# Negated scores, inverted gates, VectorE for all low parts and for even heads, and the last two down units by halves

## The chip, the cores and the metric

The kernel runs on one core of a Trainium2 chip. Its metric is the device time of one execution in microseconds (us). The engines are TensorE (PE: matmul; PEld is its weight load), VectorE (DVE), ScalarE (ACT), GpSimd (POOL) and the SyncE queue (SP), which only issues DMAs here. They run on their own and meet at semaphores.

## The reference

Two transformer blocks over 256 tokens of width 1024, all in f32. What the change touches:

```python
def masked_softmax(s, mask):
    s = jnp.where(mask, s, -1e30)
    m = jnp.max(s, axis=-1, keepdims=True)
    p = jnp.where(mask, jnp.exp(s - m), 0.0)
    return p / jnp.maximum(jnp.sum(p, axis=-1, keepdims=True), 1e-30)

# first block, 16 heads of 64; three branches (compressed, selected, window)
s = q @ k * scale + rel_bias[bucket(distance)]          # per branch
o = g[0] * (p_cmp @ v_cmp) + g[1] * (p_slc @ v_slc) + g[2] * (p_win @ v_win)
# with g = sigmoid(h @ w_gates), one value per token, branch and head
v = a * sigmoid(gate); v = depthwise conv of width 31 (v) + b     # beside it
# first block also: cross attention (4 heads of 256), a gated feed-forward layer
# second block: spatial gating, 8 heads of 64 with rope and a log-count mask,
# then 128 x 128 experts, 16 for each of 8 heads of a token:
x = x + sum over them of (gate * gelu(h @ expert_u[e])) * expert_v[e]
return rms_norm(x, final_norm_g)
```

## The kernel before

**Weights.** The kernel is a stream of 467 weight units, each 128 x 1024 f32 (512 KB), in the order of use. A ring of 4 slots holds them. SyncE loads unit u when the low part of unit u-3 is made (L328-336). ScalarE rounds it to a high part in fp32r (`ring_hi`, L1134-1139), VectorE subtracts it from the raw unit for a low part (`ring_lo`, `lo`, L1662-1669), and TensorE multiplies three times: high by high, and the two mixed products (`three`, L369-372; by rows L443-445). All activations are split in the same way (`operand_hi`, `operand_lo`).

**Who makes the low parts.** Seven units of the convolution's and q's stage (SHARED: 4 of `uconv`, 2 of `q`, 1 of `ks`) have columns 256 to 1023 of their low part made by GpSimd (`shared_lo`, L1032-1036); VectorE waits for it (`pool_lo`) and makes 256. Seven units of the gates' projections (WHOLE) are multiplied unrounded in f32 (L382) and need no low part: VectorE touches one column of them to keep the count.

**Order.** There is no scheduler: each engine's queue is written out by hand, stage after stage: memory's keys, `uconv` (16 units), `kc`, `vc`, `q`, `ks`, `kw`, the gates, `v`; then 16 units of output gates beside the 16 heads; `xv`, the convolution's and the attention's output, cross attention, feed-forward; the second block; 128 units of `expert_u` and 128 of `expert_v`; the last norm and the store.

**Convolution.** VectorE multiplies the gated values (`glu`, L1754) and makes 240 tap operations of 128 x 256 (one channel chunk of 8 and one of 30 offsets each, `tap`, L1765), spread over its queue by `some_taps(count)`: 4 behind each low part from unit `uconv`+6 on, and 6 in the steps in which a SHARED unit's low part comes up. The rest lies between the steps of the heads.

**Heads.** A loop over 8 pairs. TensorE transposes the weighted probabilities of the even head (`nsa_transposes`, L548-556, waits for `scaled`), makes the scores of the next pair (L528-541), half a gate unit, the odd head's transposes, the other half, the values (L572, L576) and a WHOLE unit (L382). VectorE adds the bias and takes the row maxima of a head (`nsa_bias`, six operations, L1792), negates them (L1809) after both banks are read, makes a low part and taps, and after ScalarE's six exponentials (`nsa_exp`, L1276-1285, which waits for that negation) turns the row sums into scales (`nsa_scale`, L1815-1818: floor, reciprocal, times gate). Heads 1 to 13 are weighed by GpSimd (L1062-1072, six operations each), heads 0, 14 and 15 by VectorE (`nsa_weigh`, L1828). GpSimd also issues the loads of the bias rows and of the second half of memory (L1075), and adds up the convolution's chunks.

**Elsewhere.** Cross attention (`x_max`, L1960-1964) and the second block's attention (`bias2`, L2116-2126) have the same negation. In the second block GpSimd scales the 8 chunks of xT by a gain (L1106) and by the row norm (L1109), 16 operations of 128 x 256; VectorE waits for them at L2197. The last stage is 128 down units (`expert_down`, L984-997) into four banks, two for each 128 rows; after the last, ScalarE squares a row block (`fin_squares`, L1640), VectorE adds, ScalarE takes the root, VectorE inverts and scales (L2354), and SyncE stores the block's 512 KB (L349).

## Time and profile before

| | |
|---|---|
| median of 3 runs | 1551.72 us (1549.52 to 1553.7) |
| profiled execution, its own time | 1551.92 us |
| its span in the trace | 1549.3 us |
| TensorE busy | 1516.1 us (98%) |
| VectorE busy | 1144.1 us (74%) |
| ScalarE busy | 813.0 us (52%) |
| GpSimd busy | 320.2 us (21%) |
| TensorE's granted clock | 9 (90% or more of full speed) in each of 40 slices |

The span is the time from the first to the last recorded instruction of one execution; the own time is what the runs measure, for that same execution. The trace is read by instruction: start, duration, engine, line of the kernel, the buffers written and read, and in brackets the idle time of the engine before it and who ended that. Rows that follow each other from one line are joined, with their count. Successive matmuls overlap, and so do VectorE's operations by some 0.08 us: the distance of two starts (the pitch) is what one of them costs.

### The profile page before, as it was taken

What the parts mean: (1) busy time and instruction counts of PE and PEld (TensorE: products, weight loads), DVE (VectorE), ACT (ScalarE), POOL (GpSimd) and SP (SyncE); (2) the same over time, 40 slices, a digit from 0 to 9 for tenths busy, and PEclk for the clock granted to TensorE, in tenths of its full rate; (3) what the DMA queues carried; (4) which work ended last, traced back from release to release, by engine and by line L of the source; (5) the groups of instructions that cost most, each with busy time, mean ns of one, the idle gap of its engine ahead of it and who ended that gap; (6) DMA issues with size and microseconds to landing.
All of it is one profiled execution on the core that took longest, in us unless ns stands there. A gap on an engine that the chain in (4) does not pass through costs nothing.

```text
span 1549.3 us, 30948 instructions
## 1 busy us (share of the span) xinstructions
PE 1516.1 (98%) x10782; PEld 1408.9 (91%) x10782; DVE 1144.1 (74%) x2383; ACT 813.0 (52%) x1456; POOL 320.2 (21%) x422
## 2 busy tenths in 40 slices
PE   8999899999999999999999999999999999999998
PEld 7998777999999998789999999999999888888886
DVE  5799888765666666867999986888888665666564
ACT  6544778654544446565655564333334445544554
POOL 2220562000100000300000005888885000000000
PEclk9999999999999999999999999999999999999999
DMA  7574433544565554533555555444445665555553
GB/s 263 172 222 148 133 107 123 170 163 134 164 202 181 182 182 145 168 110 109 168 187 177 190 188 165 137 145 139 136 139 160 195 195 191 191 192 197 192 190 108
DMA packets 70859, 257.79 MB, mean 166 GB/s; under 512 B 8272, under 2 KB 8480, under 8 KB 70528
## 3 DMA queue, kind: packets, MB, share of 16 engines
q1 hardware_dynamic: 67824, 246.97, 48.7%
q0 software_dynamic: 2960, 9.86, 2.1%
q8 instruction: 42, 0.69, 0.2%
q14 instruction: 33, 0.27, 0.1%
HBM read 254.67 MB, written 1.08 MB: 165 GB/s over the span
## 4 chain that ended last, share of the span: by engine, by line
PE 82%; DVE 10%; ACT 4%; issue 2%; POOL 1%; DMA 0%; DVEq 0%; ACTq 0%
PE bank L370 17%; PE bank L371 17%; PE bank L372 17%; PE bank L993 7%; PE bank L994 7%; PE bank L992 7%; DVE arena L1765 4%; PE bank L971 4%; DVE ring_lo L1668 3%; POOL arena L1071 1%; ACT ring_hi L1139 1%; PE bank L459 1%; ACT arena L1283 1%; PE bank L554 1%; DVE arena L1792 0%
## 5 line engine op out<-in xcount | busy, mean ns | idle before, releaser
L1668 DVE TENSOR_TENSOR ring_lo<-ring_raw,ring_hi 128x1024 fp32r<-128x1024 f32 (+1 forms) x459 | 558.1, 1219 | 182.8 <-ACT ring_hi L1139 174.7
L370 PE MATMUL bank<-operand_hi,ring_hi 128*128 128x256 f32 x2144 | 618.5, 288 | 14.0 <-DVE ring_lo L1727 7.5
L371 PE MATMUL bank<-operand_lo,ring_hi 128*128 128x256 f32 x2144 | 606.9, 283 | 0.0
L372 PE MATMUL bank<-operand_hi,ring_lo 128*128 128x256 f32 x2144 | 606.8, 283 | 0.0
L1139 ACT ACTIVATE ring_hi<-ring_raw 128x1024 fp32r<-128x1024 f32 x459 | 480.2, 1049 | 80.3 <-PE bank L372 66.2
L370 PEld LDWEIGHTS bank<-operand_hi,ring_hi 128*128 128x128 f32 x2144 | 411.3, 192 | 18.0 <-DVE ring_lo L1727 7.5
L371 PEld LDWEIGHTS bank<-operand_lo,ring_hi 128*128 128x128 f32 x2144 | 411.7, 192 | 0.3
L372 PEld LDWEIGHTS bank<-operand_hi,ring_lo 128*128 128x128 f32 x2144 | 411.2, 192 | 0.0
L1123 POOL TENSOR_SCALAR onehots<-iota_k,routeT 128x128 f32<-128x128 f32 x256 | 207.5, 827 | 230.3 <-ACT routeT L1587 193.9
L992 PE MATMUL bank<-ring_hi,hidden_hi 128*128 128x512 f32 x512 | 199.2, 389 | 0.0
L993 PE MATMUL bank<-ring_lo,hidden_hi 128*128 128x512 f32 x512 | 199.2, 389 | 0.0
L994 PE MATMUL bank<-ring_hi,hidden_lo 128*128 128x512 f32 x512 | 199.2, 389 | 0.0
L1597 ACT ACTIVATE hidden_hi<-arena 128x256 fp32r (+1 forms) x128 | 53.5, 418 | 171.4 <-PE bank L994 171.0
L2315 DVE TENSOR_TENSOR hidden_lo<-arena,hidden_hi 128x256 fp32r<-128x256 f32 x128 | 54.5, 426 | 84.5 <-ACT hidden_hi L1597 84.0
L992 PEld LDWEIGHTS bank<-ring_hi,hidden_hi 128*128 128x128 f32 x512 | 96.1, 188 | 20.1
L994 PEld LDWEIGHTS bank<-ring_hi,hidden_lo 128*128 128x128 f32 x512 | 96.1, 188 | 19.8
L993 PEld LDWEIGHTS bank<-ring_lo,hidden_hi 128*128 128x128 f32 x512 | 96.1, 188 | 19.8
L1765 DVE SCALAR_TENSOR_TENSOR arena<-arena 128x256 f32<-128x256 f32 x240 | 110.9, 520 | 0.2
L1610 ACT ACTIVATE arena<-bank 128x252 f32<-128x252 f32 (+62 forms) x63 | 17.5, 278 | 148.5 <-PE bank L372 148.5
L370 PE MATMUL bank<-hidden_hi,ring_hi 128*128 128x256 f32 x256 | 72.7, 284 | 0.1
L371 PE MATMUL bank<-hidden_lo,ring_hi 128*128 128x256 f32 x256 | 72.4, 283 | 0.0
L372 PE MATMUL bank<-hidden_hi,ring_lo 128*128 128x256 f32 x256 | 72.4, 283 | 0.0
(301 smaller groups left out, 1751.3 us busy)
## 6 DMA issues: line engine op xcount, KB each, us to landing
ring_raw<-in_stream SPq DMA_DIRECT2D x467, 512.0 KB, 3.5
arena<-bias_rows POOLq DMA_DIRECT2D x8, 384.0 KB, 4.2
arena<-in_memT SPq DMA_DIRECT2D x2, 512.0 KB, 5.0
arena<-in_xT POOLq DMA_DIRECT2D x1, 1024.0 KB, 8.0
arena<-in_w POOLq DMA_DIRECT2D x2, 512.0 KB, 9.1
arena<-in_memT POOLq DMA_DIRECT2D x1, 1024.0 KB, 5.3
out_rows<-arena SPq DMA_DIRECT2D x2, 512.0 KB, 2.6
arena<-arena POOLq DMA_DIRECT2D x4, 128.0 KB, 4.7
```

The costliest lines, as they stand in the source:

```text
L370: pe.matmul(out, wh, xh, start=start, stop=False, **kw)
L371: pe.matmul(out, wh, xl, start=False, stop=False, **kw)
L372: return pe.matmul(out, wl, xh, start=False, stop=stop, **kw)
L971: m = pe.matmul(bank[6 + q][:, j * NEXP:(j + 1) * NEXP], hot[:, q, j, :], row_hot[q][j], start=True, stop=True)
L992: pe.matmul(o, h_hi[:, par, t0], w_hi[:, slot, n0], start=False, stop=False, skip_group_check=True)
L993: pe.matmul(o, h_hi[:, par, t0], w_lo[:, slot, n0], start=False, stop=False, skip_group_check=True)
L994: m = pe.matmul(o, h_lo[:, par, t0], w_hi[:, slot, n0], start=False, stop=last, skip_group_check=True)
L1123: ins = pool.tensor_scalar(hot[:, q, j, :], iota_k[:], routeT[:, 1, token], None, ALU.is_equal)
L1139: act.activation(dst, raw[:, slot, :], ACT.Copy).then_inc(hi_ready, 1)
L1668: dve.tensor_tensor(w_lo[:, slot, 0:n], raw[:, slot, 0:n], (raw if n == 1 else w_hi)[:, slot, 0:n].bitcast(F32), ALU.subtract)\
L1765: dve.scalar_tensor_tensor(cacc[:, c, :], vconv[:, c, k:k + S], dw[:, c, k:k + 1], cacc[:, c, :], ALU.mult, ALU.add)\
L2315: dve.tensor_tensor(h_lo[:, par, :], wall[:, bass.ds(n, 1), :].rearrange("p a t -> p (a t)"), h_hi[:, par, :].bitcast(F32), ALU.subtract). ...
```

## The change

Six edits, in one version:

- The scores come out negated (q is scaled by a negative factor, masks and biases are negated), so that a minimum stands where the maximum did and is already the negated maximum that the exponential wants, whose scale is -1. The negations fall away, and ScalarE waits for the freed banks instead.
- The gates are inverted once (128 x 96); a head's scales are (floored sum x inverted gate), then the reciprocal: two operations.
- SHARED and `shared_lo` are gone: VectorE makes all low parts whole, and 4 taps stand where 6 stood.
- VectorE weighs the even heads, GpSimd the odd ones 1 to 13. Taps in the loop are 2 + 4 + 3 + 5 a pair, where they were 2 + 3 + 3 + 4.
- Block 2's scaling of xT is 8 operations of VectorE in the value phase, with the row norm and the gain in one.
- The last two down units are multiplied bank by bank (3 + 3 matmuls), each bank is reported when it is full, squared at once, and each half row block is stored by a DMA of its own (256 KB).

```diff
--- before
+++ after
@@ -31,8 +31,8 @@
 EPS = 1e-6
-NEG = -1e30
-MAX_FLOOR = -1e29
+FAR = 1e30
+MIN_CEILING = 1e29
 G, R, HD = 4, 4, 64
...
@@ -296,8 +294,6 @@
         WHOLE = [U["gattn"] + n for n in range(2, 16, 2)]
-        SHARED = [U["uconv"] + 6, U["uconv"] + 9, U["uconv"] + 12, U["uconv"] + 15, U["q"] + 3, U["q"] + 6, U["ks"] + 1]
-        SHARE = 256
         FIRST_USE = [U[n] for n in ("xk", "uconv", "xv", "pwout", "pwout", "xq", "xo", "ffn", "va", "wout2", "wq2", "expert_u")]
@@ -345,9 +341,11 @@
             for t in range(TT):
-                sp.wait_ge(fin_out, t + 1)
-                sp.dma_start(out_d[t * P:(t + 1) * P, :], fin[:, t, :]).then_inc(stored, 16)
-            sp.wait_ge(stored, 16 * TT)
+                for half in range(2):
+                    n0 = slice(half * 512, (half + 1) * 512)
+                    sp.wait_ge(fin_out, 2 * t + half + 1)
+                    sp.dma_start(out_d[t * P:(t + 1) * P, n0], fin[:, t, n0]).then_inc(stored, 16)
+            sp.wait_ge(stored, 32 * TT)
@@ -981,27 +979,40 @@
-            def expert_down(u, slot, n, par, last=False):
+            def down_half(slot, par, t, half, last=False):
+                t0 = slice(t * P, (t + 1) * P)
+                n0 = slice(half * 512, (half + 1) * 512)
+                o = bank[2 * t + half][:, :]
+                pe.matmul(o, h_hi[:, par, t0], w_hi[:, slot, n0], start=False, stop=False, skip_group_check=True)
+                pe.matmul(o, h_hi[:, par, t0], w_lo[:, slot, n0], start=False, stop=False, skip_group_check=True)
+                return pe.matmul(o, h_lo[:, par, t0], w_hi[:, slot, n0], start=False, stop=last, skip_group_check=True)
+
+            def expert_down(u, slot, n, par):
                 pe.wait_ge(lo_ready, u + 1)
...
                 for t in range(TT):
-                    t0 = slice(t * P, (t + 1) * P)
                     for half in range(2):
-                        n0 = slice(half * 512, (half + 1) * 512)
-                        o = bank[2 * t + half][:, :]
-                        pe.matmul(o, h_hi[:, par, t0], w_hi[:, slot, n0], start=False, stop=False, skip_group_check=True)
-                        pe.matmul(o, h_hi[:, par, t0], w_lo[:, slot, n0], start=False, stop=False, skip_group_check=True)
-                        m = pe.matmul(o, h_lo[:, par, t0], w_hi[:, slot, n0], start=False, stop=last, skip_group_check=True)
-                    if last and t == 0:
+                        m = down_half(slot, par, t, half)
+                m.then_inc(unit_done, 1)
+
+            def last_two(u, n):
+
+                for t in range(TT):
+                    for half in range(2):
+                        for k in range(2):
+                            if t == 0 and half == 0:
+                                pe.wait_ge(lo_ready, u + k + 1)
+                                pe.wait_ge(ehid_ready, n + k + 1)
+                            m = down_half((u + k) % RING, (n + k) % 2, t, half, last=k == 1)
                         m.then_inc(fin_bank, 1)
-                m.then_inc(unit_done, 1)
...
                     expert_down(i * RING + (u0 + k), (u0 + k) % RING, i * RING + k, k % 2)
-            for n in range(NEXP - RING, NEXP):
-                expert_down(u0 + n, (u0 + n) % RING, n, n % 2, last=n == NEXP - 1)
+            for n in range(NEXP - RING, NEXP - 2):
+                expert_down(u0 + n, (u0 + n) % RING, n, n % 2)
+            last_two(u0 + NEXP - 2, NEXP - 2)
@@ -1029,12 +1040,6 @@
-            def shared_lo(u):
-
-                s, c = u % RING, slice(SHARE, D)
-                pool.wait_ge(hi_ready, u + 1)
-                pool.tensor_tensor(w_lo[:, s, c], raw[:, s, c], w_hi[:, s, c].bitcast(F32), ALU.subtract).then_inc(pool_lo, 1)
-
             bias_rows(0)
@@ -1072,7 +1073,9 @@
                 if hh == NH - 2:
-                    pool.wait_ge(biased, NH)
+                    for b in (1, 0):
+                        emptied(pool, ("s", b, NH - 1))
+                        emptied(pool, ("s", b, NH - 2))
                     pool.dma_start(mem2, memT_d).then_inc(mem2_in, 16)
@@ -1100,13 +1103,6 @@
                 pool.dma_start(lnv[:, n, :], lnv_d[n:n + 1, :].to_broadcast([P, 512])).then_inc(lnv_in, 16)
-
-            pool.wait_ge(rows_scale, 1)
-            for c in range(KC):
-                pool.tensor_scalar(xT[:, c, :], xT[:, c, :], cols[:, G_FINAL, c:c + 1], 1.0, ALU.mult, ALU.mult).then_inc(pool_seq, 1)
-            for c in range(KC):
-                pool.wait_ge(pool_seq, 3 + c)
-                pool.tensor_tensor(xT[:, c, :], xT[:, c, :], std[:], ALU.mult).then_inc(rows_scaled, 1)
@@ -1251,7 +1247,7 @@
             for j in range(8):
-                copy_cols("q", j, qT[:, j, :], scale=HD ** -0.5)
+                copy_cols("q", j, qT[:, j, :], scale=-HD ** -0.5)
             for name, dst in (("ks", ksT), ("kw", kwT)):
@@ -1275,12 +1271,13 @@
                 s = hh % 2
-                act.wait_ge(biased, hh + 1)
+                for b in (1, 0):
+                    emptied(act, ("s", b, hh))
                 for k in parts:
...
                     v = prob[:, s, 384 * b + n0:384 * b + n1]
-                    ins = act.activation(v, v, ACT.Exp, bias=mx[:, s, k:k + 1], accum_out=sums[:, s, k:k + 1])
+                    ins = act.activation(v, v, ACT.Exp, bias=mx[:, s, k:k + 1], scale=-1.0, accum_out=sums[:, s, k:k + 1])
                 if 5 in parts:
@@ -1503,10 +1500,10 @@
                 s = h % 2
-                act.wait_ge(s2_biased, h + 1)
+                emptied(act, ("s2", h))
                 for t in range(TT):
                     v = prob2[:, s, t * S:(t + 1) * S]
-                    ins = act.activation(v, v, ACT.Exp, bias=mx[:, s, t:t + 1], accum_out=sums[:, s, t:t + 1])
+                    ins = act.activation(v, v, ACT.Exp, bias=mx[:, s, t:t + 1], scale=-1.0, accum_out=sums[:, s, t:t + 1])
                 ins.then_inc(s2_exp, 1)
@@ -1639,6 +1636,7 @@
                 for half in range(2):
+                    act.wait_ge(fin_bank, 2 * t + half + 1)
                     ins = act.activation(fsq[:, t, half * 512:(half + 1) * 512], bank[2 * t + half][:, :], ACT.Square,
@@ -1647,10 +1645,8 @@
-            act.wait_ge(fin_bank, 1)
             fin_squares(0)
             fin_std(0)
-            act.wait_ge(unit_done, UNITS)
             fin_squares(1)
@@ -1662,9 +1658,6 @@
                 n = 1 if isinstance(u, int) and u in WHOLE else D
-                if isinstance(u, int) and u in SHARED:
-                    dve.wait_ge(pool_lo, SHARED.index(u) + 1)
-                    n = SHARE
                 dve.tensor_tensor(w_lo[:, slot, 0:n], raw[:, slot, 0:n], (raw if n == 1 else w_hi)[:, slot, 0:n].bitcast(F32), ALU.subtract)\
@@ -1779,7 +1772,7 @@
                 if u >= U["uconv"] + 6:
-                    some_taps(6 if u + RING - 1 in SHARED else 4)
+                    some_taps(4)
@@ -1789,7 +1782,7 @@
                 def with_bias(out, scored, distances, n):
-                    return dve.tensor_tensor_reduce(out, scored, distances, 1.0, MAX_FLOOR, ALU.add, ALU.max, mx[:, s, n:n + 1])
+                    return dve.tensor_tensor_reduce(out, scored, distances, 1.0, MIN_CEILING, ALU.add, ALU.min, mx[:, s, n:n + 1])
@@ -1804,18 +1797,14 @@
                 ins.then_inc(bank_free[2 * s], 1)
-                for b in (1, 0):
-                    emptied(dve, ("s", b, hh))
-                dve.tensor_scalar(mx[:, s, :], mx[:, s, :], -1.0, None, ALU.mult).then_inc(biased, 1)
...
                 dve.wait_ge(exped, hh + 1)
-                after(dve.tensor_scalar(rinv[:, s, :], sums[:, s, :], 1e-30, None, ALU.max))
-                after(dve.reciprocal(rinv[:, s, :], rinv[:, s, :]))
-                r3 = rinv[:, s, :].rearrange("p (b t) -> p b t", b=3)
-                dve.tensor_tensor(r3, r3, gates[:, :, hh, :], ALU.mult).then_inc(scale_ready, 1)
+                r3, s3 = (v[:, s, :].rearrange("p (b t) -> p b t", b=3) for v in (rinv, sums))
+                after(dve.scalar_tensor_tensor(r3, s3, 1e-30, gates[:, :, hh, :], ALU.max, ALU.mult))
+                dve.reciprocal(rinv[:, s, :], rinv[:, s, :]).then_inc(scale_ready, 1)
@@ -1837,6 +1826,7 @@
             emptied(dve, ("gates", "turned"))
+            after(dve.reciprocal(gates, gates))
             nsa_scale(0)
@@ -1850,18 +1840,17 @@
                 lo_to(U["gattn"] + 2 * pair + 1 + RING)
-                some_taps(3)
+                some_taps(4)
                 if pair + 1 < NH // 2:
                     nsa_scale(2 * pair + 2)
-                    if 2 * pair + 2 == NH - 2:
-                        nsa_weigh(NH - 2)
+                    nsa_weigh(2 * pair + 2)
                 some_taps(3)
...
                     lo_to(U["gattn"] + 2 * pair + 2 + RING)
-                some_taps(4)
+                some_taps(5)
             some_taps(KC * (CONV_W - 1))
@@ -1954,14 +1943,13 @@
                 b, _ = filled[("xq", j)]
-                dve.scalar_tensor_tensor(qT[:, j, :], bank[b][:, 0:S], XHD ** -0.5, std[:], ALU.mult, ALU.mult)\
+                dve.scalar_tensor_tensor(qT[:, j, :], bank[b][:, 0:S], -XHD ** -0.5, std[:], ALU.mult, ALU.mult)\
                    .then_inc(bank_free[b], 1)
...
                 dve.wait_ge(xs, h + 1)
-                after(dve.tensor_reduce(mx[:, s, 0:TT], bank[6][:, :].rearrange("p (a b) -> p a b", a=TT), AX, ALU.max))
-                dve.tensor_scalar(mx[:, s, 0:TT], mx[:, s, 0:TT], -1.0, None, ALU.mult).then_inc(xs_max, 1)
+                dve.tensor_reduce(mx[:, s, 0:TT], bank[6][:, :].rearrange("p (a b) -> p a b", a=TT), AX, ALU.min).then_inc(xs_max, 1)
@@ -2065,9 +2053,8 @@
             dve.wait_ge(col_std, 3)
-            dve.tensor_scalar(pcolq, pcol, HD2 ** -0.5, None, ALU.mult).then_inc(col_std, 1)
-            emptied(dve, ("norm", N_2))
-            dve.reciprocal(std[:], std[:]).then_inc(rows_scale, 1)
+            dve.tensor_scalar(pcolq, pcol, -HD2 ** -0.5, None, ALU.mult).then_inc(col_std, 1)
+            rstd(("norm", N_2))
             lo_to(U["q2"] + 1 + RING)
@@ -2120,10 +2107,8 @@
                     ins = dve.tensor_tensor_reduce(prob2[:, s, t * S:(t + 1) * S], bank[4 + s][:, t * S:(t + 1) * S], lc[:, t, :],
-                                                   1.0, -3e38, ALU.add, ALU.max, mx[:, s, t:t + 1])
+                                                   1.0, 3e38, ALU.add, ALU.min, mx[:, s, t:t + 1])
                 ins.then_inc(bank_free[4 + s], 1)
-                emptied(dve, ("s2", h))
-                dve.tensor_scalar(mx[:, s, 0:TT], mx[:, s, 0:TT], -1.0, None, ALU.mult).then_inc(s2_biased, 1)
@@ -2181,6 +2166,8 @@
                         bias2(h)
+                for c in (2 * j, 2 * j + 1):
+                    dve.scalar_tensor_tensor(xT[:, c, :], xT[:, c, :], cols[:, G_FINAL, c:c + 1], std[:], ALU.mult, ALU.mult)
                 if j == 0:
@@ -2194,7 +2181,6 @@
             mix_lo(1)
-            dve.wait_ge(rows_scaled, KC)
             tail_rest("wout2", wout2_bank, O_PEER, G_NORM2)
@@ -2351,8 +2337,8 @@
                     n0 = slice(half * 512, (half + 1) * 512)
-                    ins = dve.scalar_tensor_tensor(fin[:, t, n0], bank[2 * t + half][:, :], rinv[:, 0, t:t + 1], fg[:, n0], ALU.mult, ALU.mult)
-                ins.then_inc(fin_out, 1)
+                    dve.scalar_tensor_tensor(fin[:, t, n0], bank[2 * t + half][:, :], rinv[:, 0, t:t + 1], fg[:, n0], ALU.mult, ALU.mult)\
+                       .then_inc(fin_out, 1)
```

## Rows read from the trace of the kernel before

**Rows 1.** the page, busy time by engine: us, share of span, instructions

```profile
PE 1516.1 (98%) x10782; PEld 1408.9 (91%) x10782; DVE 1144.1 (74%) x2383; ACT 813.0 (52%) x1456; POOL 320.2 (21%) x422
```

**Rows 2.** TensorE's waits: line, releaser and its line: us, times, longest

```profile
PE bank L554 <- POOL arena L1071: 4.8, 5, 1.6
PE bank L370 <- DVE ring_lo L1668: 3.4, 3, 1.5
PE bank L370 <- DVE arena L1754: 2.4, 3, 1.0
PE bank L443 <- DVE ring_lo L1668: 1.7, 2, 1.3
PE bank L443 <- DVE operand_lo L1707: 1.5, 1, 1.5
PE bank L537 <- ACT arena L1304: 1.0, 1, 1.0
PE bank L572 <- ACT arena L1312: 0.9, 2, 0.5
```

**Rows 3.** VectorE by line, 58 to 158 us: count, busy, mean ns, idle before

```profile
L1765 DVE SCALAR_TENSOR_TENSOR arena<-arena 128x256 f32<-128x256 f32 x143 | 64.8, 515 | 0.2
L1668 DVE TENSOR_TENSOR ring_lo<-ring_raw,ring_hi 128x1024 fp32r<-128x1024 f32 (+1 forms) x29 | 30.4, 1048 | 7.7 <-POOL ring_lo L1036 4.3 <-ACT ring_hi L1139 3.4
```

**Rows 4.** busy us by engine in one pair: PE, PEld, DVE, ACT, POOL

```profile
191.00:204.00 13.00, 12.37 (x100) 10.26 (x98) 10.54 (x46) 9.75 (x33) 7.22 (x13) 1.00 0.35 112
```

**Rows 5.** timeline of TensorE, block 2: start, duration, instruction, idle before

```profile
632.06 0.39 PE L445 MATMUL bank<-ring_hi,operand_lo 128*128 128x512 f32 x1
633.73 0.50 PE L443 MATMUL bank<-ring_hi,operand_hi 128*128 128x512 f32 x1 [1.29 <-DVE ring_lo L1668]
```

**Rows 6.** timeline of VectorE, 65 to 70 us

```profile
65.47 2.80 DVE L1765 SCALAR_TENSOR_TENSOR arena<-arena 128x256 f32<-128x256 f32 x4
68.20 0.41 DVE L1668 TENSOR_TENSOR ring_lo<-ring_raw,ring_hi 128x256 fp32r<-128x256 f32 x1
68.53 1.66 DVE L1765 SCALAR_TENSOR_TENSOR arena<-arena 128x256 f32<-128x256 f32 x4
```

**Rows 7.** timeline of GpSimd, the same stretch

```profile
63.98 2.82 POOL L1036 TENSOR_TENSOR ring_lo<-ring_raw,ring_hi 128x768 fp32r<-128x768 f32 x1 [6.10 <-ACT ring_hi L1139]
```

**Rows 8.** timeline of TensorE, last scores of pair 0

```profile
147.58 0.52 PE L541 MATMUL bank<-arena 64*128 64x15 f32 x8
```

**Rows 9.** timeline of VectorE, heads 0 and 1

```profile
153.80 0.27 DVE L1792 CUSTOM_DVE_ANT_0 arena<-bank,arena 128x128 f32<-128x128 f32 x1
...
156.93 0.17 DVE L1809 TENSOR_SCALAR row_max<-row_max 128x6 f32<-128x6 f32 x1
...
158.16 0.17 DVE L1815 TENSOR_SCALAR row_scale<-row_sum 128x6 f32<-128x6 f32 x1
...
158.79 1.29 DVE L1828 TENSOR_SCALAR arena<-arena,row_scale 128x128 f32<-128x128 f32 x6
```

**Rows 10.** timeline of GpSimd, one pair of heads

```profile
200.30 6.96 POOL L1071 TENSOR_SCALAR arena<-arena,row_scale 128x128 f32<-128x128 f32 x12 [5.78 <-DVE row_scale L1818]
```

**Rows 11.** timeline of VectorE, the same pair

```profile
204.03 2.33 DVE L1765 SCALAR_TENSOR_TENSOR arena<-arena 128x256 f32<-128x256 f32 x4
```

**Rows 12.** timeline of GpSimd, block 2

```profile
622.70 9.29 POOL L1109 TENSOR_TENSOR arena<-arena,std 128x256 f32<-128x256 f32 x8
```

**Rows 13.** timeline of VectorE, block 2

```profile
627.62 1.76 DVE L1668 TENSOR_TENSOR ring_lo<-ring_raw,ring_hi 128x1024 fp32r<-128x1024 f32 x1
```

**Rows 14.** timeline of TensorE, the last matmul

```profile
1541.61 0.39 PE L994 MATMUL bank<-ring_hi,hidden_lo 128*128 128x512 f32 x1
```

**Rows 15.** timeline of VectorE, the end

```profile
1544.15 0.14 DVE L2349 TENSOR_TENSOR row_scale<-row_sum 128x1 f32<-128x1 f32 x1
```

**Rows 16.** timeline of ScalarE, the end

```profile
1543.07 0.59 ACT L1642 ACTIVATE arena<-bank 128x512 f32<-128x512 f32 x1
```

**Rows 17.** the page, DMA issues: KB each, us to landing

```profile
out_rows<-arena SPq DMA_DIRECT2D x2, 512.0 KB, 2.6
```

More of the change, by code:

```diff
@@ L202, in build @@
         first_half_hi, first_half_lo = sem("first_half_hi"), sem("first_half_lo")
-        lo_ready, pool_lo = sem("lo_ready"), sem("pool_lo")
+        lo_ready = sem("lo_ready")
         unit_done = sem("unit_done")
@@ L214, in build @@
         col_std = sem("col_std")
-        rows_summed, rows_scale, rows_scaled = sem("rows_summed"), sem("rows_scale"), sem("rows_scaled")
+        rows_summed = sem("rows_summed")
         silu_done = sem("silu_done")
@@ L233, in build @@
         scores = sem("scores")
-        biased = sem("biased")
         exped = sem("exped")
@@ L267, in build @@
         s2 = sem("s2")
-        s2_biased = sem("s2_biased")
         s2_exp = sem("s2_exp")
@@ L1045, in _ @@
                 pool.dma_start(z[kv][HD:P, G, 0:CMP_BLOCK - 1], pos_d[kv][:, 1:CMP_BLOCK]).then_inc(w1_in, 16)
-            for u in SHARED[:4]:
-                shared_lo(u)
             for kv, (name, src) in enumerate((("kc", kcT), ("vc", vcT))):
@@ L1058, in _ @@
                 pool.dma_start(w1[:, kv, :, :].rearrange("p a b -> p (a b)"), w1_d[kv]).then_inc(w1_in, 16)
-            for u in SHARED[4:7]:
-                shared_lo(u)
             for hh in range(NH):
                 s = hh % 2
-                if 0 < hh < NH - 2:
+                if s and hh < NH - 1:
                     pool.wait_ge(scale_ready, hh + 1)
@@ L1226, in _ @@
                     act.wait_ge(brow_done, 1)
-                    act.activation(brow[0:NH, S:2 * S], bank[2][0:NH, 0:S], ACT.Copy).then_inc(bank_free[2], 1)
+                    act.activation(brow[0:NH, S:2 * S], bank[2][0:NH, 0:S], ACT.Copy, scale=-1.0).then_inc(bank_free[2], 1)
                 if j == 4:
@@ L1388, in x_exp @@
                     ins = act.activation(xprob[:, s, t * S:(t + 1) * S], bank[6][:, t * S:(t + 1) * S], ACT.Exp,
-                                         bias=mx[:, s, t:t + 1], accum_out=sums[:, s, t:t + 1])
+                                         bias=mx[:, s, t:t + 1], scale=-1.0, accum_out=sums[:, s, t:t + 1])
                 ins.then_inc(bank_free[6], 1)
@@ L1735, in _ @@
             dve.wait_ge(onehot_in, 32)
-            dve.memset(brow[0:NH, 0:S], NEG).then_inc(brow_sb, 1)
+            dve.memset(brow[0:NH, 0:S], FAR).then_inc(brow_sb, 1)
             dve.wait_ge(consts_in, 48)
@@ L2426 @@
     seen = (np.abs(q - k) <= 64).astype(int) + ((q - k) % 4 == 0) + ((q - k) % 16 == 0)
-    lc = np.where(seen > 0, np.log(np.maximum(seen, 1)), NEG).astype(np.float32).reshape(TT, P, S).transpose(1, 0, 2)
+    lc = np.where(seen > 0, -np.log(np.maximum(seen, 1)), FAR).astype(np.float32).reshape(TT, P, S).transpose(1, 0, 2)
     inv = (1.0 / (np.float32(10000.0) ** (np.arange(0, HD2, 2, dtype=np.float32) / np.float32(HD2)))).astype(np.float32)
```

## The prediction

> **What bounds the kernel now.** I read the page first: TensorE is busy for 1516.1 of the span of 1549.3 us [rows 1], so all that a change beside it can give back lies in the 33 us in which it is not. The profiled execution's own time is 1551.92 us, 2.6 us more than its span and 0.2 us above the median of 1551.72; the sum is made against it. Then the list of TensorE's waits [rows 2], which says who ended them: VectorE's low parts (L1668) and gated products (L1754), GpSimd's weighing (L1071, five times), and small ones on ScalarE behind them. Then VectorE by line for the 100 us from 58 to 158: it stood idle for 7.9 us, 4.3 of them behind GpSimd's parts [rows 3]; and busy time in one pair of attention heads: 10.54 of 13.00 us [rows 4]. So VectorE is full in the convolution's stage, and in the head loop it has some 2 us a pair to spare while GpSimd is late.
>
> A wait costs more than its row: the matmul after 632.06 starts 1.67 us later where the pitch is 0.23, so 1.44 us for an idle row of 1.29 [rows 5]. I add 0.15 us to each.
>
> **GpSimd's three quarters of seven low parts go to VectorE.** Each such step adds 768 columns. A quarter part costs 0.33 us (68.20 to 68.53 [rows 6]), a whole one 1.15 (it is all that stands between the negation at 156.93, a slot of 0.08, and the scale at 158.16 [rows 9]): 7 x 0.82 = +5.7 us. Against this, four taps beside GpSimd's operation of 2.82 us [rows 7] take 2.80 us and four alone 1.66 [rows 6]; the stage's 143 taps fill 64.8 us [rows 3], where at 1.66 for four they would fill 59.3: -5.5. The 4.3 us of idle time behind GpSimd's parts go. Six steps make 4 taps for 6: 12 taps x 0.40 = -4.8 us, moved behind. Together VectorE reaches the heads some 9 us earlier in its own work. How late is it today? TensorE issued the last scores of pair 0 at 147.58, VectorE took them up at 153.80 [rows 8, 9]: 5.7 us after they were there (0.5 us for the row itself), busy all the while. 9 covers 5.7, so VectorE is then at TensorE's heels and not behind it. So the waits of 100 to 158 us go: L1754 three times (2.4 + 0.45) and L1668 into L370 three times (3.4 + 0.45) [rows 2]: **-6.7 us**. The next two belong to the same lateness, since ScalarE's exponentials of pair 0 stood behind that bias: L1304 1.0, L572's first 0.5, with 0.3: **-1.8 us**. Bounds for both: 0 if VectorE is still late, 8.5.
>
> **Even heads' weights on VectorE, odd ones on GpSimd.** Today GpSimd does both heads of a pair in 6.96 us from 200.30, after 5.78 us idle [rows 10] and 0.7 us for a DMA's issue: a pair takes 13.45 us, and TensorE comes to the even head before GpSimd is done with it. VectorE does a head in six operations, 1.29 us with a pitch of 1.20 [rows 9]. Nothing of GpSimd stands before the even transposes then, and the odd head (about 3.1 of the 6.96) starts with its own scale, before the even one is through today. The five waits go: 4.8 + 0.75 = **-5.6 us**.
>
> What that costs VectorE per pair: +1.20 weighing, +0.79 (2 taps of the 12 moved, 0.40 each, plus none in the last pair), -0.36 for two negations (0.17 each [rows 9]; one slot of the pitch), -0.40 for two scales with two operations in place of three (0.63 us for three, 158.16 to 158.79 [rows 9]). Taps beside GpSimd's weighing last 2.33/4 = 0.58 [rows 11] against 0.40; with GpSimd at work for 3.1 instead of 7 us half of that goes, -0.4. Sum +0.8 to +1.2 on some 11.3 us of work (10.54 in 13.00 is 10.9 in 13.45 [rows 4], with 0.4 of gaps too short to use), so 12.1 to 12.5. TensorE without its wait needs 13.45 - 1.0 = 12.4 us. Both engines are then full, and where the taps fall just ahead of a bias or a scale, the chain bias, exponential, scale, weights comes later. I charge 0.15 us a pair, **+0.9 us**, for waits of the values (L572) or transposes, against **-0.6** for the one of today that has no other term (0.41 + 0.15; L572 stands twice, 0.9 [rows 2]). Bounds: 0 (the 1.0 us by which L1668's and the scales' idle time shrinks absorbs it) to 1.0 us a pair, 6 us, if VectorE's 12.5 grows to 13.4. The nearest row is the busy one, 10.54 of 13.00 [rows 4], so the value is near the lower end.
>
> The Trainium skill bears on this. "SBUF: State Buffer", section "Who interferes with whom", says that VectorE with two SBUF inputs and GpSimd share a port pair that one of them holds for a whole instruction, the loser waiting. Of the taps beside the low parts the trace agrees (2.80 for 1.66); beside the weighing it shows 2.33 for four, so no full block. By the page's rule the three taps or so a pair that still meet a weighing of some 0.6 us each would lose 0.3 us more each, an estimate of some 6 us in all and a time of 1540.
>
> **Negated scores and inverted gates.** The 16 + 4 + 8 negations vanish; ScalarE's exponential starts about 0.18 us sooner in each of 28 chains. It is on the path only where ScalarE waited, priced above. Inverting gates adds one reciprocal of 96 columns once, 0.35 us, ahead of the first scale; VectorE's lead covers it. GpSimd's load of the second memory block waits for freed banks instead of a count that rose 0.2 us later: nothing.
>
> **Cross values.** L443 on L1707, 1.5 us once: VectorE comes out of the loop with 3 taps left and not 5, 0.8 us earlier, less its smaller spare time: **-0.5** (0 to -1.6).
>
> **Block 2.** GpSimd's 16 operations run to 632 (622.70 + 9.29) [rows 12], and a low part beside them takes 1.76 us [rows 13], where one between other operations has a pitch of 1.15 [rows 9]. Over the 619 to 632 stretch three low parts at +0.3 to +0.5, four products slowed by 0.4 each and two scalings make about 4 us of VectorE. It was late by 1.3 and 0.5 us (L443 on L1668, 1.7 [rows 2]), so these go with 0.3 and an unlisted slip of 0.3: **-2.3 us**. What comes in their place are 8 operations of about 0.40 us in the value phase (as a tap [rows 6]), 3.2 us against 8 negations (-1.4) in a stretch where VectorE has some 12 us idle in 50; the wait of L855 at 672.5 may grow, **+0.2** (0 to 1.5).
>
> **The end.** Today both halves of the second row block end together: last matmul at 1541.61 (over at 1542.00), two squares, sum at 1544.15 [rows 14, 15]: 2.15 us, the second square from 1543.07 and 0.59 long [rows 16], 0.5 us of the rest because ScalarE was still at the first block's root. By banks only one square stands behind the last matmul, started 0.1 us after it, and the sum comes at about 1544.15 - 1543.07 - 0.2 = 0.87 us: -1.3. The last DMA carries 256 for 512 KB; the row shows 2.6 us [rows 17], of which the bytes can be at most about half: -0.3 (0 to -1). But now the last two units start as one, and unit 127's hidden part is ready only about 0.5 us after they could start (its gate waits until unit 125 is over, and split and low part take 0.42 each): +0.5 (0 to 0.9). **-1.1 us.**
>
> The skill's page "DMA: Bandwidth & Descriptors", section "Anatomy of one DMA", prices a transfer as a fixed 2.0 us plus bytes over 436 GB/s; by that the half would save an estimated 0.6 us, the sum would be 0.3 lower. The row of 2.6 us is near it.
>
> **Sum.** -6.7 -1.8 -5.6 -0.6 +0.9 -0.5 -2.3 +0.2 -1.1 = -17.5 us: 1551.92 - 17.5 = **1534.4 us**, a span of 1531.8.
>
> **Rivals.**
> 1. VectorE becomes the bound of the head loop. For: 12.1 to 12.5 us of work against TensorE's 12.4. Against: 12.5 is the upper end. At 13.2 us a pair in seven pairs it gives back 5.6: 1540 us.
> 2. The convolution's stage stays late: the low parts are whole, 5.7 us, and the taps stay at today's mean of 0.45 us (64.8/143 [rows 3]), slowed by something else than GpSimd. For: only part of them stands beside it. Against: four at 1.66 right behind four at 2.80. Half of the 8.5 and the even head's spare time are lost: 1540.
> 3. Slower: the port. If VectorE's taps and low parts in the loop are held by GpSimd's odd weights as by L1036 (2.80 for 1.66, up to 1.6 us each), and GpSimd's pass stretches too, a pair needs more than 12.4 + 17.5/7 = 14.9 us, which is the point from which the change loses; at 15.7 us it is 7 x 3.3 - 17.5 = +5.6: 1557 us. Against: four taps beside weighing, 2.33.
> 4. Most goes as forecast, and TensorE finds another late partner in the loop, ScalarE (9.75 of 13.00 [rows 4]), with exponentials of both heads in a row: 0.5 us a pair, 1538.
>
> **Chances.** Forecast 0.62 (1531 to 1537.5), rival 4 0.13, rivals 1 and 2 0.09 each, rival 3 0.02, nothing gained 0.05 (the waits change their names only). Range 1530 to 1543. About 0.3%, 4.7 us, is what a measurement of this kernel can tell from no change: faster by more 0.93, within 0.04, slower 0.03.
>
> **What would show it.** In the list of TensorE's waits L1754, L1071 and L1668 into L370 are gone or under 1 us in all; VectorE's four taps at 65 us take 1.66; the first bias starts within 1 us of the scores' end; a pair is 12.4 to 12.6 us; L443 on L1668 near 633 us is gone; the last sum stands 0.9 us behind the last matmul, and TensorE has a gap of about 0.5 us at unit 126. Wrong it is if a pair stays above 13 us, or if VectorE is still 5 us late at the first bias.

## The result and the profile after

The changed kernel takes 1533.95 us (1533.54 to 1534.65, 4 runs) against 1552.71 for the one before (1549.52 to 1553.77, 4 runs): a ratio of 0.9883 with a 95% interval of 0.9867 to 0.9899. Forecast were 1534.4 us and a span of 1531.8; the span is 1532.0. A second set on another occasion gave 1534.60 us and 0.9878 (0.9861 to 0.9894).

TensorE's waits after, with who ended them (total, times, longest), answer to [rows 2]:

```profile
PE bank L570 <- ACT arena L1309: 1.5, 4, 0.8
PE bank L634 <- ACT arena L1340: 1.0, 1, 1.0
PE bank L441 <- DVE operand_lo L1700: 0.9, 1, 0.9
PE bank L853 <- ACT arena L1482: 0.7, 1, 0.7
PE bank L986 <- DVE hidden_lo L2301: 0.4, 1, 0.4
```

GpSimd is gone from the list, and so are the gated products and the low parts. What has grown stands on ScalarE: its copies in front of the values (L570, 0.9 before) and the convolution's squares (L634, 0.3 before). VectorE over 58 to 158 us, by line, and busy times (PE, PEld, DVE, ACT, POOL) in the convolution's stage and in one pair of heads answer to [rows 3, 4]:

```profile
L1758 DVE SCALAR_TENSOR_TENSOR arena<-arena 128x256 f32<-128x256 f32 x139 | 58.2, 484 | 0.2
L1661 DVE TENSOR_TENSOR ring_lo<-ring_raw,ring_hi 128x1024 fp32r<-128x1024 f32 x29 | 35.5, 1222 | 0.4
```

```profile
58.00:100.00 42.00, 42.00 (x352) 42.00 (x351) 41.79 (x80) 21.23 (x31) 6.52 (x11) 1.00 0.64 195
189.00:201.00 12.00, 12.00 (x100) 10.34 (x96) 11.58 (x49) 9.09 (x30) 4.74 (x7) 1.00 0.34 115
```

139 taps fill 58.2 us where 143 filled 64.8, and VectorE's idle time ahead of low parts fell from 7.7 to 0.4 us. From 58 to 100 us TensorE is busy all the time; the kernel before had in the same stretch:

```profile
58.00:100.00 42.00, 39.56 (x324) 38.83 (x323) 41.79 (x79) 19.67 (x29) 9.27 (x8) 1.00 0.53 166
```

VectorE's 41.79 us are the same in both: a tap that is held up counts as busy too, so VectorE's busy share does not show what was gained, and TensorE's does. In the loop VectorE is now busy for 11.58 of 12.00 us: it has become the second full engine there.

Where the 17.3 us of the span went is read from starts of the same matmul in both traces:

| matmul | before | after | gained so far |
|---|---|---|---|
| first product behind the scores of pair 0 | 158.48 | 151.45 | 7.0 |
| values of pair 0 | 169.99 | 161.29 | 8.7 |
| even transposes of the next pairs | 243.73 | 230.53 | 13.2 |
| cross values | 264.48 | 250.56 | 13.9 |
| behind block 2's late low parts | 637.20 | 621.33 | 15.9 |
| behind the first three matmuls of unit 126 (after the change that is unit 127's first) | 1537.08 | 1521.63 | 15.45 |
| end of the span | 1549.3 | 1532.0 | 17.3 |

Traces differ in the first 13 us, before any edit: the others lie up to 0.75 us from the changed kernel's, which is itself 0.46 later than the one before. In what follows this is taken out of every distance that is said to be "from the start of the convolution on"; with it the whole gain is 17.8 us and not 17.3.

### The profile page after: what moved, and what is told of

It is laid out like the page before. It is cut to its first block, busy times and chain, and to the rows that moved or that the text cites. A ratio compares the mean times of both kernels' runs of the same rounds, so it can differ in the third digit from the quotient of the medians.

```text
span 1532.0 us, 30888 instructions
## 1 busy us (share of the span) xinstructions
PE 1513.5 (99%) x10782; PEld 1409.8 (92%) x10782; DVE 1143.9 (75%) x2384; ACT 812.7 (53%) x1456; POOL 270.9 (18%) x363
## 4 chain that ended last, share of the span: by engine, by line
PE 90%; DVE 5%; ACT 3%; issue 1%; DMA 0%; DVEq 0%; ACTq 0%
PE bank L368 18%; PE bank L369 18%; PE bank L370 18%; PE bank L986 8%; PE bank L987 8%; PE bank L988 8%; PE bank L969 4%; DVE arena L1758 1%; PE bank L441 1%; DVE ring_lo L1661 1%; PE bank L442 1%; PE bank L443 1%; PE bank L457 1%; PE bank L380 1%; ACT ring_hi L1135 1%
## 5 line engine op out<-in xcount | busy, mean ns | idle before, releaser
L1661 DVE TENSOR_TENSOR ring_lo<-ring_raw,ring_hi 128x1024 fp32r<-128x1024 f32 x459 | 562.6, 1229 | 178.2 <-ACT ring_hi L1135 175.2
L1758 DVE SCALAR_TENSOR_TENSOR arena<-arena 128x256 f32<-128x256 f32 x240 | 106.1, 503 | 0.2
```

Source lines behind the costliest of these rows:

```text
L1661: dve.tensor_tensor(w_lo[:, slot, 0:n], raw[:, slot, 0:n], (raw if n == 1 else w_hi)[:, slot, 0:n].bitcast(F32), ALU.subtract)\
L1758: dve.scalar_tensor_tensor(cacc[:, c, :], vconv[:, c, k:k + S], dw[:, c, k:k + 1], cacc[:, c, :], ALU.mult, ALU.add)\
```

## The experiments

Each undoes or adds one part; the changed kernel took 1533.95 us in the first set and 1534.60 in the second. The first four experiments ran on a third occasion, without the changed kernel beside them and with 1553.49 us for the kernel before; so where single us matter, their traces decide and not their times.

### The low parts back on GpSimd (u_lo)

```diff
+ for u in SHARED: shared_lo(u)          # GpSimd, columns 256 to 1023
- some_taps(4); loop 2 + 4 + 3 + 5
+ some_taps(6 if u + RING - 1 in SHARED else 4); loop 2 + 3 + 3 + 4
```

> The changed kernel with one part undone: GpSimd makes three quarters of seven low parts again, 6 taps in those steps, 12 taps fewer in the head loop. Theory (GpSimd's operation holds VectorE up, and the lateness of the convolution's stage is carried into the heads): TensorE's waits on the gated products and low parts between 70 and 158 us come back (6.7 us), and those of ScalarE on the first pair (1.8); the lighter loop gives back about 1 of today's 1.5 us on the values. 1541 to 1543 us, and four taps beside GpSimd's operation take 2.8 us again. Rival (the stage was late for another reason, and another of the six edits mended it): below 1536 us.

1542.62 us, span 1540.3. VectorE's timeline and TensorE's waits:

```profile
65.97 2.81 DVE L1774 SCALAR_TENSOR_TENSOR arena<-arena 128x256 f32<-128x256 f32 x4
```

```profile
PE bank L370 <- DVE arena L1763: 2.5, 3, 1.0
PE bank L370 <- ACT arena L1305: 2.3, 1, 2.3
PE bank L370 <- DVE ring_lo L1677: 2.1, 3, 1.1
PE bank L537 <- ACT arena L1314: 1.2, 1, 1.2
```

The taps beside GpSimd's operation take 2.81 again, and the waits are back: the scores of pair 1 start at 165.20 for 155.50, 9.7 us later, of which the lighter loop returns 1.5. That is 1.0 us more than the change had gained up to there; most of it lies in the wait of 2.3 us, behind ScalarE's exponentials, at the place where the kernel before waited 1.5 us for a low part. The theory holds, the rival falls.

### Even heads back on GpSimd (u_heads)

```diff
-                if s and hh < NH - 1:
+                if 0 < hh < NH - 2:
-                    nsa_weigh(2 * pair + 2)
+                    if 2 * pair + 2 == NH - 2: nsa_weigh(NH - 2)
```

> The changed kernel with one part undone: GpSimd weighs the even heads 2 to 12 too; VectorE keeps 14 taps a pair. Theory (GpSimd's 7 us for two heads end too late for the even transposes): TensorE waits for GpSimd at five or six even heads, but 0.4 us less each than before the change since no negation and one operation less of the scale stand in the chain: 5 x 0.7 us, 1537 to 1539 us. Rival (the wait came from VectorE's late scale, which the earlier convolution's stage mended): no such wait, 1533 to 1535 us.

1537.57 us. The profiled execution is the slowest of the four (1539.47 us, span 1536.6), and 3.3 us of it are TensorE's clock and no wait (last section); the other three have spans of 1533.5 to 1534.3. From the start of the convolution to the convolution's squares it lost 1.95 us:

```profile
PE bank L552 <- POOL arena L1072: 2.2, 2, 1.6
PE bank L570 <- ACT arena L1309: 1.0, 3, 0.4
```

The time falls in the expected range, but not for the expected reason. GpSimd is waited for twice and not five times, at heads 2 and 10; with the other edits in place VectorE's weighing is worth 1.9 us, not 3.5. What sets those two apart is not that GpSimd came late to them: it had stood idle for 5.8 and 3.6 us. One of GpSimd's six operations for the head ran beside a whole low part of VectorE and took as long as that, 1.3 us. Here are such an operation (of 15 columns) and its low part in the kernel before, and then all six operations of the even head at which that kernel did not wait, where the low part (216.30) started only as the last of them was ending:

```profile
202.83 1.36 POOL L1071 TENSOR_SCALAR arena<-arena,row_scale 128x15 f32<-128x15 f32 x1
202.87 1.24 DVE L1668 TENSOR_TENSOR ring_lo<-ring_raw,ring_hi 128x1024 fp32r<-128x1024 f32 x1 [0.29 <-ACT ring_hi L1139]
213.73 2.69 POOL L1071 TENSOR_SCALAR arena<-arena,row_scale 128x128 f32<-128x128 f32 x6 [5.77 <-DVE row_scale L1818]
```

This sorts every even head from 2 to 12 that GpSimd weighs in the five traces that have such heads (before, b_lo, u_heads, mixed, mixed_early). A low part falls into 16 of the 26; these take 3.8 to 4.3 us, and TensorE waits at each of them. The other 10 take 2.6 to 2.8 us, and it waits at none.

### Negation and third scale operation back (u_small)

```diff
+                dve.tensor_scalar(mx[:, s, :], mx[:, s, :], 1.0, None, ALU.mult).then_inc(biased, 1)
-                after(dve.scalar_tensor_tensor(r3, s3, 1e-30, gates[:, :, hh, :], ALU.max, ALU.mult))
-                dve.reciprocal(rinv[:, s, :], rinv[:, s, :])
+                floor; reciprocal; times gates (not inverted)
```

> The changed kernel with two small parts undone in the 16 heads: an operation in the place of the negation (times 1, ScalarE waits for it), and the scale in three operations with gates not inverted. Theory (VectorE is full in the head loop after the change, idle for some 0.3 of 12.4 us a pair): 0.76 us a pair of added work makes TensorE wait 0.4 us a pair more, 1536 to 1537 us; the waits are on the values (ScalarE's copies) and on the even head's weights. Rival (VectorE's slack absorbs it): 1533.5 to 1534.5 us.

1539.83 us, span 1537.2, with no loss of clock:

```profile
PE bank L571 <- ACT arena L1309: 4.6, 6, 1.1
PE bank L442 <- DVE operand_lo L1700: 1.3, 1, 1.3
PE bank L553 <- POOL arena L1073: 1.1, 1, 1.1
```

Both ranges missed. From the start of the convolution on it loses 4.4 us up to the values of pair 6 (242.43 for 237.30, 0.75 of it from the first 13 us): 0.63 us a pair (seven of them) for 0.76 us of added work, so that VectorE's idle 0.3 us a pair absorbed little of it. These two small edits are worth 4.4 us, more than twice the weighing.

### Block 2's scaling back on GpSimd (u_block2)

```diff
+ pool: 8 x tensor_scalar(xT, gain), 8 x tensor_tensor(xT, std)
- dve:  8 x scalar_tensor_tensor(xT, gain, std) in the value phase
```

> The changed kernel with one part undone: GpSimd scales xT in the second block by 16 operations. Theory: the low parts beside them take 1.5 to 1.76 us again, the waits of rows on low parts near 617 to 622 us come back (2.3 us, with 0.2 us given back later): 1536 us. Rival (those waits came from elsewhere): 1534 us.

1537.31 us, 1.3 over the forecast. The wait of rows on low parts is exactly back; the trace puts 2.6 us there (the same matmul at 621.33 and 623.66, and 0.27 us of another start). The profiled execution is again the slowest of its four (1541.10 us, span 1537.7), with 3.3 us of the clock behind that; the other spans are 1534.1 to 1535.5, 2.1 to 3.5 over the changed kernel's:

```profile
PE bank L441 <- DVE ring_lo L1668: 1.7, 2, 1.3
```

### The changed kernel again (after_again)

> The changed kernel once more, as the measure for the others of this group on this chip. All theories: 1533.5 to 1535 us.

1534.60 us, span 1531.7, the same waits.

### The end undone (u_tail)

```diff
- last_two(u0 + NEXP - 2, NEXP - 2)      # bank by bank, 4 DMAs of 256 KB
+ expert_down(...) twice, last=True      # row block by row block, 2 DMAs of 512 KB
```

> The changed kernel with the end undone: the last two down units one after the other, row blocks reported whole, two DMAs of 512 KB. Theory: the gap of 0.54 us at unit 126 goes, from the last matmul to the last sum it is 2.15 us instead of 0.75, the last DMA takes 0.3 to 0.6 us more: 1.1 to 1.5 us over the changed kernel. Rival (the halves only move work): within 0.3 us of it.

1536.94 us against 1534.60, spans 1533.4 and 1531.7. The last matmul starts at 1525.74 and the sum stands 2.15 us behind its end:

```profile
1525.74 0.39 PE L990 MATMUL bank<-ring_hi,hidden_lo 128*128 128x512 f32 x1
```

```profile
1528.28 0.15 DVE L2321 TENSOR_TENSOR row_scale<-row_sum 128x1 f32<-128x1 f32 x1
```

With the 0.4 us taken out by which the first 13 us differ, the end is worth 1.4 us by the spans, inside the theory; the medians are 2.3 apart, in runs that scatter by 2 to 3 us.

### VectorE weighs all heads (all_dve)

```diff
- GpSimd: six tensor_scalar for each odd head
+                    nsa_weigh(2 * pair + 3)   # and nsa_weigh(1) ahead of the loop
```

> The changed kernel with VectorE weighing the odd heads too; GpSimd weighs none and keeps its place in the order. Theory (VectorE is full, and taps beside GpSimd's weighing take 0.53 for 0.40 us): VectorE gets 1.2 us a pair more and 0.7 us less from undisturbed taps, +0.5 us a pair on TensorE, 3 us in all, 1537 to 1538 us, and five taps take 2.0 instead of 2.75 us. Rival A (the port is held for whole operations of GpSimd, so that 4 us of its work cost more than 1.2): no change or faster. Rival B (taps are slow for another reason): taps stay at 0.53, +1.2 us a pair, 1541 us.

1542.28 us, span 1540.4. Five taps of the changed kernel beside GpSimd's weighing, and five here with GpSimd idle:

```profile
193.40 2.75 DVE L1758 SCALAR_TENSOR_TENSOR arena<-arena 128x256 f32<-128x256 f32 x5
```

```profile
200.37 2.06 DVE L1751 SCALAR_TENSOR_TENSOR arena<-arena 128x256 f32<-128x256 f32 x5
```

The part on the taps holds: 0.69 us of disturbance a pair, which the absence of GpSimd gives back, and both rivals fall on it. The time was missed by 4 to 5 us. 3.3 us of the span are TensorE's clock behind a wait of 2.8 us on the values of pair 1; the rest, 5.5 us, is for the most part waits on the values, 6.7 us in all for 1.5. VectorE weighs an odd head in 1.34 us, but head 3, just ahead of that wait, in 2.77:

```profile
167.79 2.77 DVE L1810 TENSOR_SCALAR arena<-arena,row_scale 128x128 f32<-128x128 f32 x6
182.00 1.34 DVE L1810 TENSOR_SCALAR arena<-arena,row_scale 128x128 f32<-128x128 f32 x6
```

GpSimd is at work beside heads 1, 3 and 9, which take 2.28, 2.77 and 2.77 us: the same scale that starts VectorE's weighing releases GpSimd for a bias row's issue and for its sums of the convolution. In those three pairs 4.4 of the 5.5 us are lost. So this run shows that the version is slower; it does not show that GpSimd's work for odd heads is worth its disturbance where the sums stand elsewhere, which was not tried.

### A better order (both_better)

```diff
-                    for half in range(2):
-                        for k in range(2):
+  t == 0: unit 126 into banks 0 and 1, then unit 127 into banks 0 and 1
-  taps 2 + 4 + 3 + 5
+  taps 3 + 4 + 3 + 4
```

> The changed kernel with two edits of the order: for the first row block the last two units are taken as unit 126 into both banks, then unit 127 (0.68 us of work in front of the hidden part that is late), and the loop's taps are 3 + 4 + 3 + 4 instead of 2 + 4 + 3 + 5, so that VectorE takes the even head's bias up one tap earlier. Theory: the gap of 0.54 us at unit 126 goes, and the waits on the values after pair 0 (3 x 0.4 us) go or halve since ScalarE's exponentials in front of the odd head's copies start 0.4 us earlier: 1.0 to 1.7 us less than the changed kernel beside it. Rival (VectorE is the bound in the loop, so that the order of its taps moves nothing): 0.5 us less.

1533.25 us (1532.61 to 1533.65) against 1534.60 (1533.54 to 1535.62), ratio to before 0.9867 (0.9850 to 0.9883); the intervals of the two overlap, so that the order of the two rests on the traces. There the gap at unit 126 is gone (from the unit's first matmul to the next unit's it is 0.68 us and not 1.22), and 0.3 us are gained up to the convolution's squares: the waits on the values fall from 1.5 to 1.3 only, and the squares' wait grows from 1.0 to 1.4. The end of the theory holds, the loop's part is nearer to the rival.

### One part alone on the kernel before (b_lo, b_heads)

> The kernel before with one part alone: VectorE makes all low parts whole, 4 taps in each step, loop 2 + 4 + 3 + 5. Theory (the convolution's stage is worth 8.5 us by itself, and lateness is not carried through the loop): the waits of 70 to 170 us go, GpSimd's five waits at even heads stay, and 2 taps more a pair cost nothing beside them: -8 us, 1545 to 1546 us. Rival (GpSimd's waits were lateness carried on): they fall too, 1541 to 1543 us.

> The kernel before with one part alone: VectorE weighs the even heads, GpSimd the odd ones; taps and low parts as before. Theory: GpSimd's five waits go (5.6 us); VectorE's 1.2 us a pair more fit into its 2 us of idle time, with waits on the values of some 0.3 us a pair: -4 us, 1549 to 1550 us; the waits of 70 to 170 us stay. Rival (VectorE's chain of bias, negation, exponential and scale becomes the bound as soon as GpSimd isn't): the loop gives back what it gained, -1 us or less, 1552 to 1554 us.

b_lo: 1548.72 us against 1553.86, ratio 0.9966 (0.9951 to 0.9982), span 1542.7. b_heads: 1549.98 us, 0.9975 (0.9964 to 0.9986), span 1546.1. In b_heads VectorE weighs the even heads and GpSimd the odd ones; the rest of both is the kernel before. TensorE's waits, first of b_lo, then of b_heads:

```profile
PE bank L554 <- POOL arena L1061: 6.7, 6, 2.6
```

```profile
PE bank L370 <- DVE ring_lo L1668: 3.6, 4, 1.5
PE bank L572 <- ACT arena L1312: 2.6, 5, 1.1
```

b_lo wins 9.2 us up to pair 0 and loses 2.5 of them in the loop, where GpSimd's wait grows from 4.8 to 6.7 (a low part now falls into head 8 as well, so it is waited for at six heads): it is no lateness carried on, so the rival falls. But the theory is met in part only: it had the waits unchanged and 8 us won. By span b_lo wins 6.6, by time 5.1. Three of its six executions have a mean granted clock of 0.996 and spans of 1546.7 to 1548.1; the two shortest, 1542.1 and 1542.7, have 0.998 and 0.999.

b_heads removes GpSimd's five waits, and a third of that comes back on the values (0.9 to 2.6 us); it wins 3.7 us from the start of the convolution on, as the theory had it. The two alone give 10.1 us from there on; with block 2 (2.6) and the end (1.4) that is 14.1 of 17.8. u_small, which has everything but the two small edits, wins 13.3. So the last 3.6 to 4.5 us need the small edits beside the others.

### Even heads on GpSimd but for two (mixed, mixed_early)

```diff
-                if s and hh < NH - 1:
+                if 0 < hh < NH - 2 and hh not in (2, 10):
```

> The changed kernel with the two edits of the order of before (last units; taps 3 + 4 + 3 + 4), and GpSimd weighing the even heads again, but heads 2 and 10, which stood behind its sums of the convolution: there VectorE does it. Theory (with all heads' weights on GpSimd only those two were late, 2.6 us, and VectorE, which is full, is relieved of 1.2 us a pair): 1531.5 to 1532.5 us, one to two below the changed kernel with the two edits. Rival (with the even head back GpSimd is late at more heads as TensorE's waits on the values go): 1534 us or more.

> The same with taps 4 + 4 + 3 + 3: one more in front of the odd head's bias, one less in front of the even one's. Theory (what the waits on the values follow is when the even head's bias starts): 0.3 to 0.8 us below the one with 3 + 4 + 3 + 4. Rival (the odd head's chain is then as late as the even one's was): the same or up to 1 us more.

1536.93 and 1536.94 us, spans 1534.5 and 1536.1: both slower than the version they start from (both_better), and both theories fall. TensorE waits at the even head of pair 2 (mixed, then mixed_early, which waits at that of pair 6 too):

```profile
PE bank L552 <- POOL arena L1074: 1.7, 1, 1.7
```

```profile
PE bank L552 <- POOL arena L1074: 3.5, 2, 2.6
```

The idea that GpSimd is late behind its sums of the convolution, from which I chose heads 2 and 10, is wrong: it had stood idle for 4 us before head 4. Heads 4 and 6 in mixed:

```profile
178.03 4.06 POOL L1074 TENSOR_SCALAR arena<-arena,row_scale 128x128 f32<-128x128 f32 x6 [4.04 <-DVE row_scale L1809]
193.05 2.79 POOL L1074 TENSOR_SCALAR arena<-arena,row_scale 128x128 f32<-128x128 f32 x6 [7.78 <-DVE row_scale L1809]
```

A low part (179.55, 1.33 us long) made one operation of head 4 last 1.44 us. Behind the wait the clock fell as well (last section), which costs 1.7 us in both. Apart from that spot mixed gains: 1.1 us from 183.4 to 250.6 us against the changed kernel. Another place for the low part was not tried.

## Why the prediction was right, point by point

- **The convolution's stage**, -6.7 forecast, -7.5 from its start to the matmul at 158.48; the first pair -1.8 forecast, -1.7 measured. The reason held too: four taps at 64 us take 1.67 for the 2.80 of [rows 6], and VectorE takes up the first bias at 143.84, 1.1 us behind the end of its scores (142.71) and not 5.7:

```profile
63.95 1.67 DVE L1758 SCALAR_TENSOR_TENSOR arena<-arena 128x256 f32<-128x256 f32 x4
```

- **GpSimd's five waits**, -5.6 forecast, gone. But the reason was incomplete and the share of the parts wrong. I had GpSimd late by the length of its pass; the rows show that it is late at the even heads into which a low part falls, and that about 1.1 us of such a pass is the one operation that is held up. Four of the five waits were shorter than that (0.7 to 0.9 us), the fifth was 1.6. I gave the gain all to the even heads' weights; u_heads shows that with the other edits in place only two of five waits return (1.9 us net). And the step that had negations and gates on the path only "where ScalarE waited" was too small: u_small has them at 4.4 us, since VectorE is full.
- **VectorE's load of the loop**, 12.1 to 12.5 us a pair forecast; over four pairs (180.25 to 230.53) it is busy for 49.05 of 50.28 us, 12.3 of 12.6. The odd head was mis-sized: 4.04 us on GpSimd, not 3.1, because the low part now falls into it, and its taps stay slow (2.75 for five, 0.55 each). It still ends in time:

```profile
192.28 4.04 POOL L1072 TENSOR_SCALAR arena<-arena,row_scale 128x128 f32<-128x128 f32 x6 [7.58 <-DVE row_scale L1807]
```

- **New waits on the values**, +0.9 forecast, and -0.6 for the one that was to go. There are four of 1.5 us in rows; in the starts of the matmuls they cost 0.8, 0.3 and 0.2, and at pair 4, where one stood before, a wait of 0.2 stays and 0.2 is won. That is +1.0 for +0.3, so these terms are 0.7 too small.
- **Cross values** -0.5: the wait fell from 1.5 to 0.9, and the next one grew from 0.3 to 1.0, which gave 0.66 back. I had not asked what is late next there: ScalarE's squares stand behind two sigmoids of 1.9 us.
- **Inverting the gates** took 0.75 us, not 0.35, without effect on TensorE.
- **Block 2**: -2.3 forecast, -2.6 measured (629.4 to 637.2), and u_block2 puts 2.6 back. The growth of L853's wait (+0.2) did not come: 0.7 both times.
- **The end**: -1.1 forecast, -1.3 measured with the new gap of 0.54 in it (0.5 forecast):

```profile
1521.63 0.47 PE L986 MATMUL bank<-ring_hi,hidden_hi 128*128 128x512 f32 x1 [0.38 <-DVE hidden_lo L2301]
```

```profile
1527.43 0.16 DVE L2335 TENSOR_TENSOR row_scale<-row_sum 128x1 f32<-128x1 f32 x1 [0.53 <-ACT arena L1640]
```

```profile
out_rows<-arena SPq DMA_DIRECT2D x4, 256.0 KB, 2.0
```

  The last matmul is over at 1526.68, so the sum stands 0.75 us behind it (0.87 forecast). The DMA of half the bytes takes 2.0 for 2.6 us: 0.6, twice my 0.3. The Trainium skill ("DMA: Bandwidth & Descriptors", "Anatomy of one DMA") gives its fit for DMAs that GpSimd issues; worked out from it, the two would take an estimated 2.6 and 3.2 us. These are SyncE's, and the rows have 2.0 and 2.6: the difference agrees, the level lies 0.6 us under it.

The values (0.7 us) and the squares (0.7) came out worse than forecast, the convolution's stage (0.8), block 2 (0.5), the cross values (0.2) and the end (0.2) better; with the 0.46 us of the first 13 us the span missed by 0.2. The mechanisms that carry most of the sum held, the closeness of it is partly luck. Rival 1 (VectorE the bound of the loop) was nearer than its 0.09: u_small shows that it begins at the changed kernel's own load. Rival 4 is the small waits that are left. Rivals 2 and 3 fell: the taps do fall to 0.42, and in the loop those beside the weighing take 0.55 (0.58 in pair 0). The prediction's estimate of 1540 us had three taps a pair lose 0.9 us more; five of them lose 0.69 together, and VectorE's 12.3 us a pair stay below the 12.6.

By medians of times the gain is 18.8 and 19.4 us, by the two traces' spans 17.3. The spans of the other executions are on record too: those of the kernel before lie at 1550.5 to 1552.9 in the second set (median 1551.2), those of the changed kernel at 1531.7 to 1532.8 in both (median 1532.0), which makes 19.2. So the traced execution of the kernel before, with 1549.3, was a short one. In the others its mean granted clock is 0.996 to 0.999, in the changed kernel's 0.999 to 1.000; a fall as in the last section leaves that mean at 0.998 or 0.999 and costs 1.7 to 3.3 us. Such falls behind waits that the change has removed would explain it, but no trace of such an execution was kept, so this is not shown.

## What to carry to other kernels

A wait that names an engine tells who came last, not what made it late: of GpSimd's six operations a head, look at each by itself and at what VectorE does beside it. Here one low part beside it made the pass 1.1 us longer, more than was missing at four of the five heads, and an order that keeps the two apart might do as much there as moving the work (not tried). Before work is moved to a helper's neighbour, count its load by the loop's period; at 98% (49.05 of 50.28 us) 0.76 us more of it made the loop 0.63 us longer. After each removed wait, write down which engine is next in that place (the squares behind the sigmoids here).

## What the runs showed of the hardware that I had not expected

TensorE's clock halves for some 3 to 7 us behind certain gaps, in kernels that are otherwise granted the full clock. In all_dve (start and end, length, busy, count, clock, DMA) it follows an idle stretch of 2.8 us and costs 3.3 us:

```profile
175.00:177.00 2.00, 0.00 (x0) 1.00 0.00 0
177.00:179.00 2.00, 1.84 (x18) 0.84 0.31 61
179.00:181.00 2.00, 2.00 (x7) 0.50 0.53 209
181.00:183.00 2.00, 2.00 (x7) 0.50 0.00 0
183.00:185.00 2.00, 2.00 (x6) 0.50 0.54 169
185.00:187.00 2.00, 2.00 (x15) 0.95 0.68 196
```

0.50 is the lower of the two levels, 1.2 for 2.4 GHz. In mixed and mixed_early it follows the waits of 1.7 and 2.6 us at head 4, is shorter and costs 1.7 us. In u_heads, and in u_block2 alike, it comes in block 2 behind a wait of 0.7 us only, and costs 3.3 us (in u_heads the same matmul is 1.21 us later than the changed kernel's before the fall and 4.56 after it):

```profile
658.00:660.00 2.00, 1.31 (x13) 1.00 0.30 53
660.00:662.00 2.00, 2.00 (x20) 1.00 0.54 209
662.00:664.00 2.00, 2.00 (x13) 0.55 0.04 8
664.00:666.00 2.00, 2.00 (x12) 0.50 0.00 0
```

The changed kernel has the same wait at the same place and stays at 1.00; b_lo's traced execution has two gaps in a row and stays at 1.00 as well:

```profile
166.00:168.00 2.00, 0.41 (x2) 1.00 0.44 176
168.00:170.00 2.00, 0.98 (x8) 1.00 0.44 117
```

So each of the falls came behind a gap, but the same gap can pass without one, and a single time of such a kernel can be 3 us off with no wait to show for it. What decides is not shown.
